# Turning queries and keys between two column groups of the next tile's projection

## What is computed

```
def mix_inputs(x, pos, ln1, w_in):
    b, t, _ = x.shape
    p = rmsnorm(x, ln1) @ w_in
    conv_in = p[..., :CONV_CH] * jax.nn.sigmoid(p[..., CONV_CH:2 * CONV_CH])
    o = 2 * CONV_CH
    q = apply_rope(p[..., o:o + COL_Q].reshape(b, t, N_KV, Q_PER_KV, HEAD_DIM), pos)
    o += COL_Q
    kvs = []
    for _ in range(3):
        kv = p[..., o:o + COL_KV].reshape(b, t, N_KV, 2, HEAD_DIM)
        kvs.append(jnp.stack([apply_rope(kv[..., 0, :], pos), kv[..., 1, :]], axis=-2))
        o += COL_KV
    gates = jax.nn.sigmoid(p[..., o:o + COL_GATE].reshape(b, t, N_KV, Q_PER_KV, 3))
    return conv_in, q, kvs[0], kvs[1], kvs[2], gates
...
        a, q, ckv, skv, wkv, g = mix_inputs(xp, pos_p, ln1[l], w_in[l])
        conv_out = conv_module(jnp.pad(a, ((0, 0), (CONV_W - 1, 0), (0, 0))), *conv_w)
        att = nsa_prompt(q, ckv, skv, wkv, g, pos_p, cmp_w)
        xp = merge_and_ffn(xp, conv_out, att, *ffn_w)
```

## Time and profile before

| | |
|---|---|
| median of 3 executions | 1574.31 us (1573.7 to 1576.0) |
| the profiled execution's own time | 1570.66 us |
| its span in the trace | 1569.0 us |
| mean granted TensorE clock over the span | 0.944 |
| busy shares | PE 89%, PEld 52%, DVE 44%, ACT 24%, POOL 13% |

### The profile page before, as it was taken

One profiled execution on the slowest core, in us unless ns is written; L12 is line 12 of the kernel. 1 busy time (PEld: TensorE's weight loads), 2 busy tenths in 40 slices (PEclk: granted clock), 3 DMA queues, 4 the chain that ended last, 5 costly groups with the idle time before them and its releaser, 6 DMA issues. The chain is left out here.

```text
span 1569.0 us, 22334 instructions
## 1 busy us (share of the span) xinstructions
PE 1394.6 (89%) x7470; PEld 821.5 (52%) x7470; DVE 685.8 (44%) x1413; ACT 370.6 (24%) x802; POOL 211.5 (13%) x363
## 2 busy tenths in 40 slices
PE   5999999889889898886999759999999999999950
PEld 3665544489655666555555434455444455444420
DVE  3398688671488777766245450011010011111027
ACT  4000011142366555552111101111111111111112
POOL 0000122153230000024000010111111111111101
PEclk9999999989689999998999869999999999999985
DMA  8500111174443000019311078999999999999935
GB/s 294 214 40 1 41 54 60 55 261 156 148 148 92 28 2 15 1 51 288 118 54 54 34 286 326 397 409 407 416 414 403 417 389 401 403 404 396 404 131 227
DMA packets 99400, 330.94 MB, mean 211 GB/s; under 512 B 12391, under 2 KB 58856, under 8 KB 76467
## 3 DMA queue, kind: packets, MB, share of 16 engines
q1 hardware_dynamic: 83626, 292.88, 48.0%
q0 software_dynamic: 15696, 37.09, 6.8%
HBM read 313.11 MB, written 31.62 MB: 220 GB/s over the span
## 5 line engine op out<-in xcount | busy, mean ns | idle before, releaser
L2118 PE MATMUL ps<-arena 128*128 128x512 f32 x544 | 238.2, 596 | 0.1
L2118 PEld LDWEIGHTS ps<-arena 128*128 128x128 f32 x544 | 102.2, 190 | 135.5 <-issue 135.5
L569 DVE SCALAR_TENSOR_TENSOR arena<-arena 128x1024 f32<-128x1024 f32 x120 | 151.4, 1312 | 1.2
L402 PE MATMUL ps<-arena 128*128 128x512 f32 (+1 forms) x384 | 141.2, 528 | 0.0
L2127 PE MATMUL ps<-arena 128*64 128x256 f32 x1088 | 121.2, 381 | 0.0
L356 PE MATMUL ps<-arena 128*128 128x352 f32 x384 | 115.9, 464 | 4.5 <-issue 4.1
L2171 PE MATMUL ps<-arena 128*128 128x512 f32 x272 | 119.5, 592 | 0.0
L1186 ACT ACTIVATE arena<-ps,arena 128x640 f32<-128x640 f32 (+7 forms) x128 | 89.7, 701 | 108.5 <-DVE arena L1262 103.6
L1584 PE MATMUL ps<-arena 128*128 128x512 f32 x256 | 114.6, 602 | 0.4 <-ACT arena L1693 0.4
L2231 DVE TENSOR_TENSOR arena<-arena,ps 128x512 f32<-128x512 f32 x17 | 11.7, 688 | 225.0 <-PE ps L2118 225.0
L402 PEld LDWEIGHTS ps<-arena 128*128 128x128 f32 x384 | 72.5, 190 | 66.7 <-issue 61.2
(11 more groups left out here) (367 smaller groups left out, 1588.2 us busy)
## 6 DMA issues: line engine op xcount, KB each, us to landing
arena<-in_w_gate SPq DMA_DIRECT2D x34, 2048.0 KB, 8.6
arena<-in_w_up SPq DMA_DIRECT2D x34, 2048.0 KB, 14.5
arena<-in_w_down SPq DMA_DIRECT2D x34, 2048.0 KB
arena<-in_cache_cmp SPq DMA_DIRECT2D x80, 128.0 KB, 2.6
arena<-in_x_prompt SPq DMA_DIRECT2D x16, 512.0 KB, 5.7
arena<-in_cache_sel SPq DMA_DIRECT2D x64, 128.0 KB, 2.9
arena<-scratch_y SPq DMA_DIRECT2D x16, 512.0 KB, 5.6
arena<-in_cache_cmp POOLq DMA_DIRECT2D x48, 128.0 KB, 2.7
```

The lines of the kernel that those rows point to most:

```text
L402: mm = pe.matmul(ps[:n, b + o // 512, 0:w], xT[:, k, t * P:t * P + n], w_tm[:, k, o:o + w], start=(k == 0), stop=(k == KT_ - 1))
L569: ins = dve.scalar_tensor_tensor(o, i, dw[:, c, j:j + 1], o, ALU.mult, ALU.add)
L2118: mm = pe.matmul(ps[:, bank, :], xgT_l[:, k, :], w[LARGE][:, k, :], start=(k == 0), stop=(k == KT_ - 1))
```

## The change

For tiles 1 to 7, `turn(t - 1)` (six transposes, without the doubled rows) moves in between the second and the third column group of tile t. The transposes of the doubled rows become a function of their own, `turn_doubled`, which stays behind the third group. At tile 8 all stays in the old order. ACT's `turn_copy(t - 1)` moves ahead of tile t's copies, for tiles 1 to 7 too. No instruction is added or removed.

```
-                    if t < NQ:
-
-                        pe.wait_ge(sem("qk_copied"), t + 1)
-                        pe.wait_ge(sem("doubled"), t + 1)
-                        for o in range(0, 512, P):
-                            mm = pe.transpose(ps[:, 6, o:o + P], xin[:, t % 2, o:o + P], ident)
-                        mm.then_inc(sem("cmp_turned"), 1)
+
+                def turn_doubled(t):
+                    pe.wait_ge(sem("qk_copied"), t + 1)
+                    pe.wait_ge(sem("doubled"), t + 1)
+                    for o in range(0, 512, P):
+                        mm = pe.transpose(ps[:, 6, o:o + P], xin[:, t % 2, o:o + P], ident)
+                    mm.then_inc(sem("cmp_turned"), 1)
...
                         for o, w in ((0, 512), (512, 512), (1024, COLS_TM - 1024)):
+                            if t >= 1 and o == 1024:
+                                turn(t - 1)
                             for k in range(KT_):
...
                     mm.then_inc(sem("tm_projected"), 1)
+                    if t == NQ:
+                        turn(t - 1)
                     if t >= 1:
-                        turn(t - 1)
+                        turn_doubled(t - 1)
...
                     n, b = rows(t), 3 * (t % 2)
+                    if 1 <= t < NQ:
+                        turn_copy(t - 1)
                     act.wait_ge(sem("tm_projected"), t + 1)
...
-                    if t >= 1:
+                    if t == NQ:
                         turn_copy(t - 1)
```

## The result

The changed kernel runs in 1560.8 us (median of 4 executions, 1557.88 to 1561.98), the kernel before in 1574.16 us. The ratio is 0.9914 with a 95% interval of 0.9897 to 0.9931: 13.4 us faster, where 11.9 us were forecast.

A forecast was written before the change was run, and what follows sets the result against it. The prediction took PE to bound the loop, stalled 1.65 us per tile; 7 tiles x 1.70 us = 11.9 us off the median 1574.3 us gave 1562.4 us, range 1558.6 to 1566.7 us.

The forecast's parts named there:

- PE sets the pace of the loop, and stops at L390: Tile loop: PE is busy 18.82 of 20.47 us and idles 1.65 us per tile before the doubled rows.
- The third column group covers the copy, with 2.2 us to spare: Between the six transposes and L390: 3.75 us of matmuls cover ACT's copy, about 2.2 us to spare.
- 1.70 us per tile: Per changed tile: at most 1.81 us can go, less 0.10 us for two changes; period 18.77 us.
- the upper bound of 1.81 us: L383 to L390: 2.03 us between starts, less 0.22 us for two transposes, is the most a tile can gain.
- Seven of eight stalls: Tiles 1 to 7 lose their stall, tile 8's, the longest, stays: 7 x 1.70 = 11.9 us.
- The new wait of `turn(7)` for L527, 0.4 us, absorbed: Tile 8: turn(7) waits about 0.4 us for keep_as_page(6), absorbed because ACT reads its result later.
- DVE is next: Tile loop: DVE's 18.74 us of work for tile 3 still fits the 18.77 us period, nearly without idle time.
- The next block starts 11.9 us earlier and keeps it: Block's end: the barrier comes 11.9 us earlier, with no transfer found that holds the next block at its old time.
- The costlier changes: Rival, chance 0.12: both new transpose-matmul changes cost 0.44 us per tile, gain 9.6 us, 1564.7 us.
- the drain bare at each change: Within the rival of chance 0.12: about 175 ns bare at each transpose-matmul change, gain about 1.46 us a tile, 1564.1 us.
- The slower case: Rival, chance 0.03: the shift lays 30 us more at half clock, 15 us of loss, 1577.4 us.
- The time of a missing cover: At L390 without any cover a 1.2 us stall remains: gain 3.2 us, 1571.1 us; gain mostly lost, chance 0.05.

The follow-up runs named there:

- e1_pe_alone: Changed kernel with ACT's turn_copy back behind the tile's own copies, so only TensorE's new order remains: 1584.07 us, ratio 1.0059 to the kernel before.
- e3_cover_1: Changed kernel with the turn ahead of the third group's last matmul, so one matmul covers the copy: 1563.27 us, ratio 0.9937.
- e6_six_pieces: Changed kernel with the six transposes issued one by one ahead of six matmuls of the second group: 1561.11 us, ratio 0.9910.
- e7_dve_more: Changed kernel with one more unused reduction of 1024 columns per tile on DVE, tiles 1 to 6: 1560.66 us, ratio 0.9911.
- e2_act_alone: Kernel before with only ACT's new order, turn_copy ahead of the tile's copies, TensorE's list untouched: 1568.27 us, ratio 0.9969.
- e9_filled: e1_pe_alone with two unused 512-column matmuls before the doubled rows in tiles 1 to 7: 1575.83 us, ratio 1.0027 to the kernel before.
- e11_tail_sp_out: e8_tail with the sample rows' three output DMAs issued by SyncE in place of GpSimd: 1561.04 us, ratio 0.9919.
- e8_tail: Changed kernel with the samples' queries turned into bank 5, without the cmp_copied wait, behind the convolution state's transposes: 1563.11 us, ratio 0.9927.

## Why the prediction was right, point by point

- *PE sets the pace of the loop, and stops at L390.* Right: with the stall gone the loop's window is full, and adding work to DVE did not slow it.
- *The third column group covers the copy, with 2.2 us to spare.* Right, and the spare is 2.7 us by the changed kernel's rows. The prediction took 1.2 us for start and copy where its own terms, 0.1 and 0.90 us, give 1.0 us. e1_pe_alone and e3_cover_1 show both conditions, a free ACT and a cover of 1.34 us.
- *1.70 us per tile.* This is the term that was mis-sized: 1.87 us were measured (20.47 - 18.60), 7 x 1.87 = 13.1 us for 11.9 us. What was wrong in it is the price of a change between transposes and matmuls. I read 0.05 us of it from the four transposes of L390, 0.49 us against 0.44 us for L380. That was the cost of starting again after a stall: in the changed kernel L390, without a stall, takes 236.58 - 236.15 = 0.43 us. So these 0.05 us went with the stall, and the two new changes, priced at 0.10 us, cost nothing (e6_six_pieces). For the same reason the upper bound of 1.81 us was too low.
- *Seven of eight stalls.* Right; tile 8's is 1.60 us where it was 2.04 us, since 0.39 us of it now lie in the wait before it.
- *The new wait of `turn(7)` for L527, 0.4 us, absorbed.* Right: 0.39 us (the prediction's own terms, 5.39 less 5.1 us, give 0.3 us), and ACT reads the turned rows at 299.00 us, behind its own copies.
- *DVE is next.* Right in the order, but it no longer fits as the prediction had it: in the changed kernel its rotations of tiles 3 to 6 start 18.8 us apart (219.45, 238.29, 257.08 and 275.85), with no idle time before them, for a period of 18.60 us. So DVE falls behind by about 0.2 us a tile and makes it good in tile 6's lighter work, before tile 7. e7_dve_more confirms that a larger lag costs PE nothing in the loop.
- *The next block starts 11.9 us earlier and keeps it.* It starts 12.5 us earlier in the two profiles, although the loop's first matmul came 0.56 us later in that of the changed kernel (144.67 against 144.11 us): 13.1 - 0.56 = 12.5 us. That the medians differ by 13.4 us, so near the 13.1 us of the loop, says little by itself: the interval of their ratio reaches 2.7 us to either side.
- *The rivals.* The costlier changes are refuted by e6_six_pieces, and with them the drain bare at each change that I had worked out from the Trainium skill ("TensorE: Matmul & The Clock Gate", section "Single matmul latency"). The slower case, by half-clock stretches, did not come: the mean granted clock is 0.946 against 0.944. But such stretches can arise in this loop. In e1_pe_alone half clock cost what I had said half clock costs, 0.5 us per us.
- *The time of a missing cover,* 0.45 us x 7 = 3.2 us of gain: e2_act_alone measured 0.69 us x 7 = 4.8 us. I had set the stall at 1.2 us then; it is 0.96 us.

## What to carry to other kernels

When an engine hands something over and waits for the copy to come back, move other work of its own between the two, and then look at the copying engine's list: here the copy stood behind work that could not start before the cover was over, and moving TensorE's side alone made the kernel slower by 0.6%, while ACT's side alone gained 0.3%. Measure the cover needed from the trace (here 1.34 us), and place the hand-over anywhere that leaves it. A transition cost read beside a stall may belong to the stall. And before an engine's work is moved to free a barrier, look at when every engine reaches it: here two engines were within 0.5 us of each other, and freeing one alone gave nothing.

## What the runs showed of the hardware

- TensorE's granted clock fell from full (2.4 GHz) to half (1.2 GHz) behind 3 of the 7 stalls of 2.30 us in e1_pe_alone, each time for 3.4 us in which PE was busy throughout; such a stall cost 2.30 us and 1.7 us more behind it. It fell behind none of the 1.65 us stalls of before nor the 0.58 us ones of e9_filled, but it did at the end of a stall of 1.60 us at tile 8 of the changed kernel. Which stalls it follows, these runs do not settle.
- Transposes and float32 matmuls mix at their own paces, 0.11 us and 0.43 us a record, with nothing lost at a change; the four transposes of L390 took 0.49 us behind a stall and 0.43 us without one.
- 16 register loads from SBUF on SyncE took about 9 us (295.22 to 304.36 in e11_tail_sp_out), long enough to hold the DMAs behind them.
- GpSimd's DRAIN ahead of the block's barrier took 2.77 us behind its own DMAs (the changed kernel, e8_tail) and 2.64 us in the three kernels that took the last of them away; SP's took 0.007 us.
